# Hybrid decoder block on one core: the first token tile's key selection moved ahead of a weight split, exponentials moved ahead of another, one weight chunk taken by halves, and the output gate computed token by token

## The reference

```python
h = rmsnorm(x, norm_mix)
aq, ak, av, iq, iw, ik, bq, bf, bi, bg, ga, gb = split(h @ w_in)       # 12 parts, 5928 columns
y_a = dsa_sparse_attention(aq, ak, av, iq, iw, ik, rel_bias)           # 64 keys a query, by an index score
o_b = hgrn2_chunkwise(bq, bf, bi, lb)                                  # gated linear recurrence
o_b = rmsnorm(o_b, hgrn_norm) * silu(bg)                               # the output gate
merged = sigmoid(ga) * (y_a @ w_up_a) + sigmoid(gb) * (o_b @ w_up_b)
x = x + merged @ w_out
x = x + moe_ffn(rmsnorm(x, norm_ffn))                                  # top 4 of 32 experts, clamped SwiGLU
out = rmsnorm(x, norm_final)
```

## Time and profile before

| | |
|---|---|
| Time, 3 runs | 1138.43, 1137.52, 1138.41 us; median 1138.41 |
| The profiled execution, its own time | 1137.58 us |
| Its span in the profile | 1135.8 us |
| Busy: TensorE, VectorE, ScalarE, GpSimd | 1106.5 us (97%), 330.3 (29%), 212.3 (19%), 16.2 (1%) |
| DMA | 443.07 MB, 390 GB/s over the span |
| Granted TensorE clock | 0.998 of full speed |

### The profile page before, as it was taken

How to read it: one execution, slowest core, us unless ns; L and a number is a source line. 1 busy time by engine, 2 the same in 40 slices (tenths; PEclk the granted TensorE clock), 3 DMA queues, 4 the chain that set the end, 5 groups by cost and what they waited for, 6 DMA issues and landing times.

```text
span 1135.8 us, 15281 instructions
## 1 busy us (share of the span) xinstructions
PE 1106.5 (97%) x6338; PEld 488.9 (43%) x6338; DVE 330.3 (29%) x566; ACT 212.3 (19%) x297; POOL 16.2 (1%) x25
## 2 busy tenths in 40 slices
PE   8999999999999999999999999999999999999997
PEld 5998999733333333333333333333333333333332
DVE  4789758441111111111111111111111111111112
ACT  4454434220111101010101010101010101010002
POOL 0020000000000000000000000000000000000000
PEclk9999999999999999999999999999999999999999
DMA  9967647999999999999999999999999999999996
GB/s 323 233 214 263 203 153 270 426 393 424 422 434 428 433 432 428 430 434 425 430 436 429 430 435 426 427 432 429 429 432 431 430 432 430 430 431 432 428 422 237
DMA packets 41110, 443.07 MB, mean 390 GB/s; under 512 B 3929, under 2 KB 7673, under 8 KB 23033
## 3 DMA queue, kind: packets, MB, share of 16 engines
q1 hardware_dynamic: 38920, 439.66, 93.3%
q10 hardware_dynamic: 2160, 2.98, 0.8%
HBM read 441.19 MB, written 1.44 MB: 390 GB/s over the span
## 4 chain that ended last, share of the span: by engine, by line
PE 75%; DMA 21%; DVE 1%; ACT 1%; SPq 1%; issue 0%; POOLq 0%; POOL 0%; ACTq 0%
PE psum L980 27%; PE psum L1012 16%; DMA ring<-in_w_gu 16%; PE psum L945 4%; DMA qk_silu<-in_w_down 4%; PE psum L960 4%; PE psum L991 2%; PE psum L598 2%; PE psum L607 2%; PE psum L600 2%; DMA ring<-in_w_in 1%; PE psum L574 1%; PE psum L999 1%; PE psum L569 1%; PE psum L954 1%; PE psum L570 1%
## 5 line engine op out<-in xcount | busy, mean ns | idle before, releaser
L980 PE MATMUL psum<-ring,hT_region 128*64 128x512 f32 x1536 | 343.1, 595 | 13.3 <-DMA ring<-in_w_gu 12.9
L980 PEld LDWEIGHTS psum<-ring,hT_region 128*64 128x64 f32 x1536 | 107.2, 137 | 242.1 <-issue 220.7
L1707 DVE TENSOR_SCALAR hT_region<-psum 128x512 f32<-128x512 f32 x32 | 22.1, 692 | 398.9 <-PE psum L980 398.9
L1012 PE MATMUL psum<-qk_silu,hT_region 128*64 128x512 f32 x512 | 116.9, 598 | 1.8 <-DMA qk_silu<-in_w_down 1.8
L980 PE MATMUL psum<-sig_vb,hT_region 128*64 128x512 f32 x512 | 112.6, 592 | 0.0
L1303 ACT ACTIVATE x_sb<-hT_region 128x512 f32<-128x512 f32 x32 | 20.1, 629 | 421.6 <-DVE hT_region L1707 421.6
L1656 DVE TENSOR_TENSOR hT_region<-psum,tiny 128x512 f32<-128x512 f32 x32 | 22.1, 692 | 204.2 <-PE psum L954 204.2
L945 PE MATMUL psum<-work,idx_region 128*64 128x512 f32 x256 | 68.8, 617 | 0.0
L980 PEld LDWEIGHTS psum<-sig_vb,hT_region 128*64 128x64 f32 x512 | 36.8, 137 | 73.1 <-issue 73.1
L1371 DVE TENSOR_TENSOR slot_r<-ring,slot_r 128x2048 fp32r<-128x2048 f32 (+1 forms) x21 | 60.2, 2874 | 19.3 <-ACT slot_r L1148 12.3
L960 PE MATMUL psum<-x_sb,idx_region 64*128 64x512 f32 x256 | 63.6, 615 | 0.0
(11 more groups left out here) (279 smaller groups left out, 1037.6 us busy)
## 6 DMA issues: line engine op xcount, KB each, us to landing
ring<-in_w_gu SPq DMA_DIRECT2D x39, 4096.0 KB, 26.2
qk_silu<-in_w_down SPq DMA_DIRECT2D x31, 2048.0 KB, 17.7
sig_vb<-in_w_gu SPq DMA_DIRECT2D x13, 4096.0 KB, 26.4
ring<-in_w_down SPq DMA_DIRECT2D x16, 2048.0 KB, 29.3
ring<-in_w_gu SPq DMA_DIRECT2D x16, 2048.0 KB, 12.7
hg<-in_w_down SPq DMA_DIRECT2D x16, 2048.0 KB, 31.0
ring<-in_w_in SPq DMA_DIRECT2D x12, 1024.0 KB, 5.2
sig_vb<-in_w_gu SPq DMA_DIRECT2D x6, 2048.0 KB, 15.3
```

The source lines that it names most:

```text
L980: last = mm(psum[half * 64:half * 64 + 64, b, :], xgT_sb[:, a:a + SLOTS], slot_gu(p, c, b, half)[:, jj], start=(j == 0), stop=(j == NJ - 1 ...
L1012: last = mm(psum[half * 64:half * 64 + 64, 2, :], actT_sb[:, a:a + SLOTS], slot4(DOWN_HOME[p][m // 4])[:, m % 4, half * 512:(half + 1) * 5 ...
L1707: v.tensor_scalar(gate_sb, psum[:, 0, :], LIMIT, None, ALU.min).then_inc(gate_ready, 1)
```

## The change

The change has four parts and what belongs to them.

1. Chunk 1 is loaded, rounded and subtracted by halves, and multiplied as `rows_T`, half by half. The small operations on the recurrence's lower bound move behind the first half's low part on VectorE, and behind both high parts on ScalarE.
2. `top_keys` for the first token tile follows that for the second at once. The low part of chunk 5 is made inside it, ahead of its round 3.
3. ScalarE takes the exponentials of the second token tile first, then chunk 8's first high half, then the exponentials of the first tile.
4. Chunk 7 is multiplied in the token form, and so the gate is applied before the transposes, by VectorE, one bank at a time, in turn with ScalarE's squares. VectorE also does the scaling that GpSimd did. After the transposes ScalarE makes the high part with the gain as its scale, head by head, and VectorE the low part. The load of the second half of expert 0's `w_down` waits for the gating instead of for the finished result.

The diff, without the declarations of semaphores:

```diff
@@ -83,7 +83,9 @@
-    return chunk - 1 if chunk <= SPLIT else SPLIT - 1 + 2 * (chunk - SPLIT)
+    if chunk == 1:
+        return 0
+    return chunk if chunk <= SPLIT else SPLIT + 2 * (chunk - SPLIT)
@@ -391,6 +393,11 @@
                 w = IDX_W if n == 0 else 512
+                if n == 1:
+                    for half in range(2):
+                        j = slice(4 * half, 4 * half + 4)
+                        sp.dma_start(slot_in(n)[:, j, :], w_in_v[:, j, c0:c0 + w]).then_inc(first_loaded[half], 16)
+                    continue
                 sp.dma_start(slot_in(n), w_in_v[:, :, c0:c0 + w]).then_inc(w_loaded[s], 16)
@@ -426,7 +433,7 @@
-            sp.wait_ge(yb_ready, 1)
+            sp.wait_ge(o_gated, 2)
             load_down(0, 0, 1)
@@ -608,7 +615,7 @@
-            def rows_tok(n, half):
+            def rows_tok(n, half, amid=None):
@@ -617,6 +624,8 @@
                         mm(dst, hT_low[:, j, toks], high[:, j, :], start=False, stop=False, skip_group_check=True)
+                    if r == 0 and amid:
+                        amid()
                 low_part(n, half)
@@ -626,16 +635,20 @@
             def project(n, half, amid=None):
-                if half == 0 or n >= SPLIT:
+                if half == 0 or n >= SPLIT or n == 1:
                     pe.wait_ge(high_ready, parts_before(n) + half + 1)
...
                 if n < SPLIT:
-                    last = half_tok(n, half) if ORDER[n] == "av" else half_T(n, half)
+                    if n == 1:
+                        last = rows_T(n, half)
+                    else:
+                        last = half_tok(n, half) if ORDER[n] == "av" else half_T(n, half)
                     if half:
...
                 else:
-                    last = rows_tok(n, half) if ORDER[n] == "bi" else rows_T(n, half, amid)
+                    rows = rows_tok if ORDER[n] in ("bi", "bg") else rows_T
+                    last = rows(n, half, amid)
                     last.then_inc(half_used[slot_of(n)][half], 1)
@@ -830,7 +843,7 @@
-                pe.wait_ge(yb_ready, 1)
+                pe.wait_ge(y_b_low_ready, 1)
                 for bank in (6, 7):
@@ -1143,8 +1155,12 @@
                 s = slot_of(n)
-                if n < SPLIT:
-                    act.wait_ge(w_loaded[s], 16 * turn_of(n))
+                if n == 1:
+                    act.wait_ge(first_loaded[half], 16)
+                    words = slice(half * HALF, (half + 1) * HALF)
+                    f(slot_r[high_slot(n)][:, words], ring[:, s, words], ACT.Copy).then_inc(high_ready, 1)
+                elif n < SPLIT:
+                    act.wait_ge(w_loaded[s], 16 * (turn_of(n) - (s == 1)))
                     f(slot_r[high_slot(n)][:, :], ring[:, s, :], ACT.Copy).then_inc(high_ready, 1)
@@ -1156,9 +1172,10 @@
+            take_high(1, 0)
+            take_high(1, 1)
             act.wait_ge(lb_shifted, 1)
             f(tiny_lb, tiny_lb, ACT.Exp).then_inc(lb_exp, 1)
-            take_high(1)
@@ -1192,8 +1209,9 @@
             f(hf, proj(5), ACT.Sigmoid).then_inc(evacuated[1], 1)
-            take_high(8, 0)
             for n, r in enumerate((1, 0)):
+                if n:
+                    take_high(8, 0)
                 act.wait_ge(max_ready, n + 1)
@@ -1238,13 +1256,17 @@
             act.wait_ge(o_mm, 1)
-            f(hk, banks(6, 8), ACT.Square).then_inc(o_squared, 1)
+            f(hk[:, 0:512], psum[:, 6, :], ACT.Square).then_inc(o_squared, 1)
+            act.wait_ge(o_gated, 1)
+            f(hk[:, 512:1024], psum[:, 7, :], ACT.Square).then_inc(o_squared, 1)
             act.dma_start(wr_sb, w_router[0].rearrange("(p j) e -> p (j e)", j=NJ)).then_inc(router_w_in, 16)
...
             f(sig_b[:, 1024:2048], proj(11), ACT.Sigmoid).then_inc(evacuated[1], 1)
-            act.wait_ge(yb_ready, 1)
-            f(y_b_high, hf, ACT.Copy).then_inc(y_b_high_ready, 1)
+            act.wait_ge(yb_mm, 1)
+            for h in range(BH):
+                cols = slice(h * S, (h + 1) * S)
+                f(y_b_high[:, cols], banks(6, 8)[:, cols], ACT.Copy, scale=g_hgrn[:, h:h + 1]).then_inc(y_b_high_ready, 1)
             take_high(13, 1)
@@ -1354,10 +1376,6 @@
-            dve.wait_ge(params_in, 64)
-            link(v.tensor_tensor(lbm, lb0, lb1, ALU.max))
-            v.tensor_tensor(lb0, lb0, lbm, ALU.subtract)
-            v.tensor_tensor(lb1, lb1, lbm, ALU.subtract).then_inc(lb_shifted, 1)
             for r in range(NT):
@@ -1367,11 +1385,16 @@
                 dve.wait_ge(high_ready, parts_before(n) + half + 1)
-                words = slice(0, CHUNK) if n < SPLIT else slice(half * HALF, (half + 1) * HALF)
+                words = slice(0, CHUNK) if 1 < n < SPLIT else slice(half * HALF, (half + 1) * HALF)
                 v.tensor_tensor(slot_r[slot_of(n)][:, words], ring[:, slot_of(n), words],
...
-            take_low(1)
+            take_low(1, 0)
+            dve.wait_ge(params_in, 64)
+            link(v.tensor_tensor(lbm, lb0, lb1, ALU.max))
+            v.tensor_tensor(lb0, lb0, lbm, ALU.subtract)
+            v.tensor_tensor(lb1, lb1, lbm, ALU.subtract).then_inc(lb_shifted, 1)
+            take_low(1, 1)
             dve.wait_ge(lb_exp, 1)
@@ -1388,7 +1411,7 @@
-            def top_keys(n, r, sc, relu, between=None):
+            def top_keys(n, r, sc, relu, between, amid):
@@ -1398,7 +1421,7 @@
                 for k in range(TOPK // 8):
-                    if k == 5 and between:
+                    if k == amid:
                         take_low(between)
@@ -1412,9 +1435,8 @@
             dve.wait_ge(consts_in, 16)
-            top_keys(1, 1, score1, relu1, between=4)
-            take_low(5)
-            top_keys(2, 0, score0, relu0)
+            top_keys(1, 1, score1, relu1, 4, 5)
+            top_keys(2, 0, score0, relu0, 5, 3)
@@ -1524,21 +1546,24 @@
+            dve.wait_ge(o_mm, 1)
+            v.tensor_tensor(hq[:, 512:1024], psum[:, 7, :], silu_g[:, 512:1024], ALU.mult).then_inc(o_gated, 1)
             dve.wait_ge(o_squared, 1)
-            v.tensor_reduce(o_ss, hk.rearrange("p (g e) -> p g e", e=BD), AX.X, ALU.add).then_inc(o_squares, 1)
+            v.tensor_tensor(hq[:, 0:512], psum[:, 6, :], silu_g[:, 0:512], ALU.mult).then_inc(o_gated, 1)
+            dve.wait_ge(o_squared, 2)
+            link(v.tensor_reduce(o_ss, hk.rearrange("p (g e) -> p g e", e=BD), AX.X, ALU.add))
+            v.tensor_scalar(o_ss, o_ss, 1.0 / BD, EPS, ALU.mult, ALU.add).then_inc(o_squares, 1)
+            dve.wait_ge(o_gated, 2)
             dve.wait_ge(o_rs_ready, 1)
             o3 = hq.rearrange("p (g e) -> p g e", e=BD)
-            v.tensor_tensor(o3, banks(6, 8).rearrange("p (g e) -> p g e", e=BD),
-                            bc(o_rs.unsqueeze(2), [P, NT * BH, BD]), ALU.mult).then_inc(o_normed, 1)
+            v.tensor_tensor(o3, o3, bc(o_rs.unsqueeze(2), [P, NT * BH, BD]), ALU.mult).then_inc(o_normed, 1)
             take_low(13, 0)
-            dve.wait_ge(yb_mm, 1)
             for h in range(BH):
                 cols = slice(h * S, (h + 1) * S)
-                last = v.scalar_tensor_tensor(hf[:, cols], banks(6, 8)[:, cols], g_hgrn[:, h:h + 1], silu_g[:, cols],
-                                              ALU.mult, ALU.mult)
-            last.then_inc(yb_ready, 1)
-            dve.wait_ge(y_b_high_ready, 1)
-            v.tensor_tensor(y_b_low, hf, y_b_high.bitcast(F32), ALU.subtract).then_inc(y_b_low_ready, 1)
+                dve.wait_ge(y_b_high_ready, 2 * (h // 2) + 2)
+                last = v.scalar_tensor_tensor(y_b_low[:, cols], banks(6, 8)[:, cols], g_hgrn[:, h:h + 1],
+                                              y_b_high[:, cols].bitcast(F32), ALU.mult, ALU.subtract)
+            last.then_inc(y_b_low_ready, 1)
@@ -1796,7 +1821,7 @@
             pool.wait_ge(o_squares, 1)
-            root(o_rs, o_ss, BD, NT * BH, o_rs_ready)
+            g.tensor_tensor(o_rs, o_ss, minus_half.broadcast_to([P, NT * BH]), ALU.pow).then_inc(o_rs_ready, 1)
             pool.wait_ge(half_used[slot_of(UP_A)][1], half_turn(UP_A))
```

## The result

The changed kernel took 1143.41 us (median of 5 runs, 1143.15 to 1145.12) against 1137.68 us of the kernel before beside it: ratio 1.0047, 95% interval 1.0036 to 1.0058. It is slower by 5.7 us. The forecast was 1140.0 us, with a range from 1136.0 to 1141.5: slower was right, and the time lies outside the range.

What follows compares the result with a forecast made beforehand. The prediction took the expert weights' DMA stream, started by TensorE's work before 232 us, as the bound. Terms -1.69 + 3.77 - 0.64 + 0.15 = +1.59 us on 1137.58 gave 1139.2, as a median 1140.0 us; range 1136.0 to 1141.5.

Steps and rivals of the forecast that it cites:

- What bounds the kernel: Expert stage: DMA stream at constant rate; what TensorE gains or loses before 232 us moves the end by the same amount.
- Chunk 1 by halves: Chunk 1: TensorE no longer waits for VectorE's low part; -1.69 us, bounds 0 and -1.7.
- The gate chunk by tokens: Chunk 7: 48 products of 512 columns replace 96 of 256; -0.64 us.
- The gate before the transposes: Output gate: work added ahead of the last transposes shows in full; +0.15 us, bounds 0 and +0.7.
- The exponentials: Exponentials ahead of chunk 8's high half: cost and gain 0, hidden by TensorE's own products; bounds 0 and +1.
- The selection: Chunk 5: GpSimd's addition holds VectorE, so the low part comes late and TensorE stands; +3.77 us, bounds 0 and +4.5.
- Rival 2: VectorE's chain from chunk 3's load has no slack, so later loads or GpSimd lengthen the stall; 1142.0 at 2 us; chance 0.14.
- 1: First tile's selection: GpSimd does not hold VectorE in line 1397, no stall; -2.2 us, 1136.2; chance 0.22 (with 4).
- 3: First tile's selection: GpSimd and VectorE take turns, stall of 1.5, sum -0.7 us, 1137.7; chance 0.06.
- 4: The change does what it looks like: selection 4.3 us ahead all the way, same time as 1; chance 0.22 together.

Runs made afterwards that it cites:

- the gate alone: The kernel before with only the edits that touch the output gate (gate chunk by tokens, gate multiplied in before the transposes): 1138.04 us.
- one round first: The changed kernel with chunk 5's low part behind the first of the eight rounds of maxima instead of the third: 1141.56 us.
- the addition later: The changed kernel with GpSimd's first addition to the bias waiting also for chunk 5's low part: 1137.14 us.
- the halves alone: The kernel before with the second chunk's halves and nothing else of the change: 1138.25 us.
- selection alone: The kernel before with only the second part of the change, chunk 5's low part made inside the first tile's key selection: 1141.96 us.
- later without gate: The changed kernel without any of the output gate's parts, and with GpSimd's first addition held back until chunk 5's low part is done: 1136.64 us.

## Why the prediction was wrong

**What bounds the kernel** held: the stream's rate did not change and the end moved with TensorE's work ahead of it. "By the same amount" did not quite. The request moved by 4.96 us, the span by 5.4. Most of the difference arises at one place, around 501 us, at a down projection that waits for its weights:

```profile
501.74 3.65 PE L1012 MATMUL psum<-qk_silu,hT_region 128*64 128x512 f32 x16 [0.20 <-DMA qk_silu<-in_w_down]
```

```profile
507.05 3.65 PE L1024 MATMUL psum<-qk_silu,hT_region 128*64 128x512 f32 x16 [0.56 <-DMA qk_silu<-in_w_down]
```

```profile
502.68 3.65 PE L1013 MATMUL psum<-qk_silu,hT_region 128*64 128x512 f32 x16 [1.60 <-DMA qk_silu<-in_w_down]
```

```profile
PE psum L1024 <- DMA qk_silu<-in_w_down: 3.8, 3, 1.6
```

The first three are before, after and the gate alone. The last is the total of such waits with one round first: 3.8 us in three, where the kernel before has 1.8 in two. The wait around 501 us is 0.20, 0.56, 1.60 and 1.62 us in the four. Of the gate alone's 0.79 us nothing is left behind it (its requests there are 0.9 us later than before), and one round first, 0.65 us behind at the request, is 2.7 us behind. With the addition later 0.35 of 1.94 us are given back there, with the halves alone 0.65 of 1.50. With one trace of each kernel, it stays open whether this wait belongs to the kernel or to the execution.

**Chunk 1 by halves**, -1.69: right in kind, and in size for this pair of traces (-1.75). But the wait of 1.44 us that it takes away was that of one execution: in two other kernels with the same chunk 1 it was 0.52 and 0.84, so against such an execution the gain is 0.5 to 0.9 us smaller. And made alone, with the request 1.50 us earlier, it is not in the time (0.9995 to 1.0013).

**The gate chunk by tokens**, -0.64: right (-0.58; 48 products at 0.226 are 10.86 us and not 10.88, which changes the term by 0.02). **The gate before the transposes**, +0.15: right in kind; the wait that it adds is 0.20 us, its price in the pair of runs 0.22.

```profile
177.13 1.09 PE L841 MATMUL psum<-cst,hg 128*128 128x128 f32 x8 [0.20 <-DVE hg L1559]
```

**The exponentials**, 0 with bounds 0 and +1: 0 with the addition later, about 0.9 us where the selection is late. The bounds held; the cover was VectorE's time in hand, and I had named only TensorE's products.

**The selection**, +3.77: the mechanism was right to the row, and the step that failed is what a stand costs TensorE. The prediction put it at the length of the stand, 3.67 us, "with 0.10 for the block behind a wait". Measured: a stand of 4.23 us and 2.79 us more, because the clock fell to its lower level and stayed there for nearly all of the 32 products behind; 7.02 us in place of 3.77. I had only the wait of 1.44 us, with products at full pace behind it, and took its price for a longer one. The stand itself came out 0.56 us longer than the 3.67, because the chain ran later: the mask comes at 62.43 instead of 61.87. 0.36 of it is chunk 3's load, the rest chunk 4's, whose high part ends at 54.70, 0.2 us after VectorE wants it.

```profile
37.26 3.62 ACT L1164 ACTIVATE slot_r<-ring 128x4096 fp32r<-128x4096 f32 x1 [10.71 <-DMA ring<-in_w_in]
51.07 3.63 ACT L1164 ACTIVATE slot_r<-ring 128x4096 fp32r<-128x4096 f32 x1 [7.51 <-DMA ring<-in_w_in]
```

Rival 2 had named that chain; what made the loads land later I did not test.

**The rivals.** 1, 3 and 4 are out: VectorE was held for one whole operation (4.69 us). The change does what it looks like only with the addition later.

**Outside the span.** I assumed what lies around the span unchanged. It was 1.82 us before and 2.25 after, and that is 0.4 of the 5.7 us. All ten kernels with the gate chunk by tokens have a median of 2.2 to 2.9 us, the four without it (before, selection alone, halves alone, later without gate) 1.8 to 1.9. So it comes with that edit, not with the halves' semaphores or loads; by what in it is open, and the profile begins too late or ends too early to show it.

The whole: 4.96 at the request, 0.4 in the expert stage, 0.4 outside the span, together 5.8, as the two profiled executions differ (1143.41 less 1137.58); the medians differ by 5.7.

## What to carry to other kernels

Before an operation is put into another engine's idle gap, look at what that gap was sparing: here GpSimd's addition, which held a VectorE operation with two SBUF inputs for its whole length. Price a stand of TensorE by its length and by the clock behind it, and take that price from a stand of the same length; where it can't be avoided, products that nobody reads can keep the clock up. Compare the start of the stretch as well as its end before a difference between two traces is put down to an edit, and hold it against the times of all executions. A gain of a tenth of a percent ahead of a stream of loads must still pass each place where the loads are just in time.

## What the hardware showed that I had not expected

- TensorE's granted clock fell from 1.00 to 0.50 (2.4 to 1.2 GHz) during a stand of 4.1 us, and products of 256 columns then followed each other in 0.213 us instead of 0.12 for some 6 us. Behind stands of 2.0 and 2.4 us it stayed at 1.00, behind one of 2.1 us it fell, 1.2 us after the products had begun again.
- A `scalar_tensor_tensor` with two inputs in SBUF waits for a whole operation of GpSimd (0.35 becomes 4.69 us); in pieces of 0.75 to 0.80 us the two take turns. A `tensor_scalar` of 128x128 with one input in SBUF was held too, 1.38 instead of 0.23 us. The rounds of maxima beside the same addition were not.
- The time outside the span is not the same for all kernels: with the gate chunk by tokens (48 products in place of 96) its median was 2.2 to 2.9 us, without it 1.8 to 1.9. In the pair that differs in that form alone it was 2.66 against 1.91 us, though the outputs of that pair differ.
- TensorE's wait in chunk 1, for a chain that starts with a load, was 0.52, 0.84 and 1.44 us in three kernels with the same code up to there.
